# Expert matrices in 8 KB pieces, and a gathered block turned by sixteen 64x64 products with the identity

## What is computed

```python
def hier_moe(x, wg, bg, we, be, w1, w3, w2):
    ...   # route: each token gets 2 of 64 experts and two gates
    def expert_block(args):
        xb, e = args                      # xb: rows of tokens of expert e
        h = jax.nn.silu(xb @ w1[e]) * (xb @ w3[e])     # 1024 -> 256
        return h @ w2[e]                               # 256 -> 1024
    ys = lax.map(expert_block, (xs, blk_e)).reshape(R, D)
    out = jnp.zeros_like(xt).at[row_tok].add(ys * row_w[:, None])
```

## Time and profile before

| | |
|---|---|
| time, median of 3 runs | 3161.15 us (3158.59 to 3164.65) |
| span of the profiled execution | 3159.2 us |
| TensorE busy | 2918.6 us, 92% |
| TensorE weight loads busy | 2268.3 us, 72% |
| VectorE busy | 1399.3 us, 44% |
| ScalarE busy | 920.2 us, 29% |
| GpSimd busy | 608.3 us, 19% |
| DMA | 600.31 MB, mean 190 GB/s |

### The profile page before, as it was taken

One profiled execution on the slowest core, in us unless ns is written; L12 is line 12 of the kernel. 1 busy time (PEld: TensorE's weight loads), 2 busy tenths in 40 slices (PEclk: granted clock), 3 DMA queues, 4 the chain that ended last, 5 costly groups with the idle time before them and its releaser, 6 DMA issues.

```text
span 3159.2 us, 42475 instructions
## 1 busy us (share of the span) xinstructions
PE 2918.6 (92%) x17571; PEld 2268.3 (72%) x17571; DVE 1399.3 (44%) x2437; ACT 920.2 (29%) x1714; POOL 608.3 (19%) x534
## 2 busy tenths in 40 slices
PE   8999999999999999999999898888699997998884
PEld 7659999998888778888787555555577775555552
DVE  5634323343444543233544453323588844533234
ACT  4543313232222333142322121111335721211112
POOL 1404101120111131021100442222000002522220
PEclk9999999999999999999998899999899998999998
DMA  4012222222222222233225899999622139999996
GB/s 141 27 54 68 94 94 85 90 90 71 71 84 76 68 71 99 88 100 101 79 81 214 348 407 409 410 409 409 249 80 77 57 119 364 405 408 410 409 409 278
DMA packets 272213, 600.31 MB, mean 190 GB/s; under 512 B 32648, under 2 KB 177603, under 8 KB 255627
## 3 DMA queue, kind: packets, MB, share of 16 engines
q1 hardware_dynamic: 247552, 569.47, 47.9%
q0 software_dynamic: 23968, 27.93, 2.7%
q10 hardware_dynamic: 490, 0.08, 0.0%
HBM read 607.75 MB, written 39.89 MB: 205 GB/s over the span
## 4 chain that ended last, share of the span: by engine, by line
PE 86%; DVE 5%; issue 4%; ACT 2%; DMA 2%; POOL 1%; SPq 0%; ACTq 0%; DVEq 0%; POOLq 0%
PE ps L101 80%; PE ps L104 6%; DVE sb_tmpA L118 1%; DVE sb_arena L126 1%; DMA sb_arena<-in_exp_w_dram 1%; DVE sb_arena L118 1%; DVE sb_ws L118 1%; POOL sb_arena L118 0%; DMA sb_arena<-y_rows 0%; DVE sb_tmpA L129 0%; DMA sb_arena<-x_rows,sb_smallu 0%; ACT sb_arena L112 0%; ACT sb_hs L108 0%; ACT sb_hT L108 0%; DMA sb_arena<-in_x_dram 0%
## 5 line engine op out<-in xcount | busy, mean ns | idle before, releaser
L101 PE MATMUL ps<-sb_hs,sb_ws 128*128 128x264 f32 (+1 forms) x6384 | 1106.5, 335 | 17.2 <-ACT sb_hs L108 7.5
L101 PEld LDWEIGHTS ps<-sb_hs,sb_ws 128*128 128x128 f32 x6384 | 971.0, 190 | 148.2 <-issue 16.5
L118 DVE TENSOR_TENSOR sb_ws<-sb_ring,sb_ws 128x1024 fp32r<-128x1024 f32 x279 | 370.5, 1332 | 428.0 <-ACT sb_ws L112 427.5
L112 ACT CAST sb_ws<-sb_ring 128x1024 fp32r<-128x1024 f32 x279 | 290.8, 1046 | 333.6 <-PE ps L101 318.1
L101 PE MATMUL ps<-sb_arena 128*64 128x256 f32 (+18 forms) x1652 | 347.6, 420 | 26.6 <-issue 19.8
L101 PE MATMUL ps<-sb_br,sb_ws 128*128 128x264 f32 (+1 forms) x2304 | 367.4, 321 | 0.0
L101 PEld LDWEIGHTS ps<-sb_br,sb_ws 128*128 128x128 f32 x2304 | 332.4, 188 | 34.2 <-issue 0.5
L101 PE MATMUL ps<-sb_ring,sb_arena 128*64 128x256 f32 (+2 forms) x1506 | 284.0, 450 | 25.4 <-issue 22.6
L108 ACT ACTIVATE sb_arena<-ps 64x256 f32<-64x256 f32 (+6 forms) x188 | 73.8, 403 | 756.5 <-PE ps L101 733.8
L101 PEld LDWEIGHTS ps<-sb_arena 128*64 128x64 f32 (+6 forms) x1652 | 197.9, 160 | 128.7 <-issue 69.9
L104 PEld LDWEIGHTS ps<-sb_cst,sb_arena 128*128 128x128 f32 (+2 forms) x912 | 139.4, 209 | 170.6 <-DVE sb_arena L118 82.2
(11 more groups left out here) (198 smaller groups left out, 2602.7 us busy)
## 6 DMA issues: line engine op xcount, KB each, us to landing
sb_ring<-in_exp_w_dram SPq DMA_DIRECT2D x113, 1024.0 KB
sb_hx<-in_exp_w_dram SPq DMA_DIRECT2D x92, 1024.0 KB
sb_arena<-in_exp_w_dram SPq DMA_DIRECT2D x66, 1024.0 KB
sb_wx<-in_exp_w_dram SPq DMA_DIRECT2D x66, 1024.0 KB
sb_ring<-in_mlp_w_dram SPq DMA_DIRECT2D x64, 1024.0 KB
sb_hT<-in_exp_w_dram SPq DMA_DIRECT2D x47, 1024.0 KB
sb_ring<-in_od_w_in_dram SPq DMA_DIRECT2D x24, 1024.0 KB
sb_ring<-in_conv_w_in_dram SPq DMA_DIRECT2D x12, 1024.0 KB
```

The costliest lines, as they stand in the source:

```text
L101: return self.e.matmul(o, l, r, start=start, stop=stop, skip_group_check=True)
L112: return self.e.copy(o, i)
L118: return self.e.tensor_tensor(o, a, b, op)
```

## The change

The rows of the first and third matrices are dealt to the partitions differently: partition p now holds rows 8p to 8p+7, one run of 8 KB, in `moe_load` and in `over_sp`. To match, the turned block must have value 8p+o of a token in partition p. The values with p below 64 are in the upper 64 partitions of the gathered block and the others in the lower 64, so `turn_rows` takes for each o two 64x64 blocks (every eighth column) and multiplies each by the 64x64 identity: 8 x 2 ordinary products (`e.mm`) instead of 4 transposes (`e.tp`). `xgT`, `up_mm`, `columns_dve` and the loads of gains and biases follow the new order; their sizes stay.

```diff
--- before.py
+++ after.py
@@ -607,8 +607,8 @@
                     *grow_in.land())
             for l in range(2):
                 for i, name in enumerate(GROWS[0:2]):
-                    e.dma(sm[:, 384 + 16 * l + 8 * i:392 + 16 * l + 8 * i].rearrange("p (h o) -> p h o", h=2),
-                          A[name][l].rearrange("(h p o) -> p h o", h=2, o=4)).then_inc(*grow_in.land("all"))
+                    e.dma(sm[:, 384 + 16 * l + 8 * i:392 + 16 * l + 8 * i],
+                          A[name][l].rearrange("(p o) -> p o", o=8)).then_inc(*grow_in.land("all"))
             e.wait_ge(*dve_emptied["lut"])
             e.dma(Bd.rearrange("h (a b) -> h a b", a=2), lut).then_inc(*lut_out.land("all"))
 
@@ -2246,7 +2246,7 @@
 
         ar.at = base
         xg = ar.take(NG, 512)
-        xgT = ar.take(2, 4, 128)
+        xgT = ar.take(2, 8, CAP)
         hs = ar.take(2, 256)
         hhT = ar.take(2, 2, CAP)
         yy = ar.take(3, 512)
@@ -2363,7 +2363,7 @@
             if c == 2:
                 src, dst = W.rearrange("(p o) n -> p o n", o=2), v.rearrange("p (o n) -> p o n", o=2)
             else:
-                src, dst = W.rearrange("(h p o) n -> p h (o n)", h=2, o=4), v.rearrange("p (h n) -> p h n", h=2)
+                src, dst = W.rearrange("(p o) n -> p o n", o=8), v.rearrange("p (o n) -> p o n", o=8)
             e.dma(dst, src).then_inc(*wsignal(l, n).land(("moe", l, n)))
 
         for i in range(NSLOT):
@@ -2407,10 +2407,12 @@
             return q
 
         def turn_rows(e, units, key, src):
-            v = src.rearrange("s (p o) -> s o p", o=4)
+            v = src.rearrange("s (p o) -> s o p", o=8)
             u = units.take(e, key)
-            for o in range(4):
-                q = e.tp(u[:, 128 * o:128 * o + 128], v[:, o, :], ident)
+            for o in range(8):
+                for p in (0, CAP):
+                    q = e.mm(u[p:p + CAP, CAP * o:CAP * o + CAP], v[p:p + CAP, o, :], ident[p:p + CAP, p:p + CAP],
+                             True, True)
             return q
 
         def up_mm(e, units, key, xs, w1, w3):
@@ -2420,7 +2422,7 @@
             for k in range(8):
                 for c, w in enumerate((w1, w3)):
                     q = e.mm(u[CAP * c:CAP * c + CAP, 512 * c:512 * c + 256],
-                             xs[:, k % 4, CAP * (k // 4):CAP * (k // 4) + CAP], w[:, k, :], k == 0, k == 7)
+                             xs[:, k, :], w[:, k, :], k == 0, k == 7)
                     if k == 7:
                         ends.append(q)
             return ends
@@ -2656,9 +2658,8 @@
 
         def columns_dve(e, l, step, dst, src):
 
-            dst, src = (v.rearrange("p o (h s) -> p o h s", h=2) for v in (
-                dst, src[:, 0:512].rearrange("p (o n) -> p o n", o=4)))
-            g, b = (grid(GX[:, l, 8 * i:8 * i + 8], (1, 4), (4, 2), (0, CAP)) for i in range(2))
+            src = src[:, 0:512].rearrange("p (o s) -> p o s", o=8)
+            g, b = (grid(GX[:, l, 8 * i:8 * i + 8], (1, 8), (0, CAP)) for i in range(2))
             e.tt(dst, src, g, ALU.mult).then_inc(*step.mark())
             e.wait_ge(*step.now)
             return e.tt(dst, dst, b, ALU.add)
@@ -2772,11 +2773,7 @@
             x = e.e.value_load(over_of(l)[0:1, j:j + 1], min_val=0, max_val=63)
             for c in range(3):
                 W = EW[l][c][bass.ds(x, 1), :, :] if e.real else EW[l][c][0:1, :, :]
-                if c == 2:
-                    i = e.dma(ovw[:, c, :], W.rearrange("a (p o) n -> (a p) (o n)", o=2))
-                else:
-                    i = e.dma(ovw[:, c, :].rearrange("p (h m) -> p h m", h=2),
-                              W.rearrange("a (h p o) n -> p (a h) (o n)", h=2, o=4))
+                i = e.dma(ovw[:, c, :], W.rearrange("a (p o) n -> (a p) (o n)", o=2 if c == 2 else 8))
                 i.then_inc(*ovw_in[l].land(j))
 
         def over_pe(e, l, j):
```

## The result

The kernel with the change takes 3183.83 us (median of 4 runs, 3182.43 to 3185.06), the kernel before beside it 3160.02 (3158.59 to 3164.65): a ratio of 1.0071, 95% interval 1.0057 to 1.0084. The profiled executions say the same: 3181.8 us of span against 3159.2. The change makes the kernel slower by 0.7%.

A forecast was written before the change was run, and what follows sets the result against it. Transfers were taken to bound both expert loops, TensorE a close second. Per loop -9.1 + 0.7 = -8.4, two loops -16.8: span 3159.2 to 3142.4, plus 1.95 gives 3144.3 us; range 3138 to 3165.

The forecast's parts named there:

- What bounds the kernel: Both expert loops: weight transfers at 405 to 410 GB/s set the end; TensorE, 6.38 us per expert, is a close second.
- Part 1: First and third matrices' loads: 8 KB pieces save fixed packet cost, about 10 ns a packet, 9.1 us per loop.
- Rival B: Weight transfers: bytes, not packets, set the rate, so little or nothing is saved; 3162.6 down to 3156 us, chance 0.13.
- Part 2: Turn of the gathered block: sixteen products take 1.16 us, +0.48 per expert (6.86 us), hidden where transfers bind.
- so 0.06 for 64: Turn's weight loads: transposes' 0.12 us per 128 strided columns halved, giving 0.06 us per pair of product instructions.
- Rival C: Turn's loads: a step of 8 elements costs half as much again, 0.09 per pair; 3143 to 3160 us, chance 0.04.
- Rival A: Turn: row halves do not run side by side, TensorE binds at 7.82 us per expert; 3202.5 us, chance 0.16.
- The limit of TensorE: First loop: last up product could start at 1757.6 + 63c, c being us per expert; gain gone at 7.46.
- Part 3: Start of each loop: nothing hides the slower half-clock turn, costing 0.5 to 0.9 us, taken as 0.7 per loop.
- the forecast's own case: Whole kernel: pairs at 0.06 us, transfers still set the loops' ends; 3144.3 us, range 3139 to 3150, chance 0.67.
- One answer: Parts judged certain: VectorE's columns pass keeps 0.69 us; gain loads, overflow blocks and arena size cost nothing.

The follow-up runs named there:

- e1_pieces_only: Kernel before with only the 8 KB pieces of first and third matrices, four transposes kept: 3148.41 us, ratio 0.9956.
- e15: e16 with sixteen real products with the identity in place of its eight transposes, same 64 rows and 128 strided columns: 3641.06 us.
- e16: Changed kernel, but whole 4 KB rows gathered into 64 partitions, four blocks ahead, turned by eight transposes of 64 rows by 128 step-8 columns: 3183.25 us, ratio 1.0064.
- e3_step1: Changed kernel, but each 64x64 product takes 64 adjacent columns as weights in place of every eighth: 3152.54 us, ratio 0.9976.
- e9_halves_in_turn: Changed kernel with the sixteen products reordered, the eight of partitions 0-63 first, then those of 64-127: 3495.32 us in one run.
- e6_eight_transposes: Changed kernel with eight transposes of 128 rows by 64 step-8 columns in place of the products, plus VectorE passes: 3154.15 us, ratio 0.9981.

## Why the prediction was wrong

**What bounds the kernel**: right. Transfers came first, TensorE second; from 6.38 us per expert it had some 1.1 us to the point where the gain is gone (7.46 by the prediction's working). The change crossed that margin.

**Part 1**: right in kind, a fifth too large. 415 GB/s came where 417 was foretold, the weights' queue has 16988 packets in place of 26532. Before and after give one line: (279.7 - 181.7) / (7,223 - 4,579) = 0.037 ns per byte and 12 ns per packet, next to the prediction's 9.1 to 11.6. Alone it gave 14.8 of 18.2 us. Rival B is refuted. The Trainium skill, "DMA: Bandwidth & Descriptors", section "Why small descriptors are slow (HBM only)", has about 3 cycles per packet, an estimated 3.5 ns, which would have given 3.2 us per loop; e1_pieces_only gained 6.0 and 8.8.

**Part 2, the step that failed**: "so 0.06 for 64". The 0.12 us of a transpose was read rightly, but carried to another kind of instruction. Per strided column a real fp32 product pays twice what the transpose pays (e15 against e16); so a pair costs 0.12 and not 0.06, the turn 2.07 and not 1.16, an expert 7.77 and not 6.86. The other row used, 54 ns from the index products, has adjacent columns; e3_step1 shows that it was right for those (0.06 per pair, 6.78 us per expert). Rival C named the cause, the step of 8, and priced it at half as much again with a chance of 0.04; it is the true case with twice the price. Rival A gave the right pace (7.82) for a reason that e9_halves_in_turn refutes, and held the 0.16 that C should have had.

**The limit of TensorE**: 1757.6 + 63c was too strict. The first experts run into the routing's wait, which ends at the same time whatever the turn costs: the fifth up product starts at 1780.50 + 2.07 = 1782.57, before at 1782.50. Only 58 full steps follow: 1782.5 + 58c + 5.7 = 2238.9, measured 2238.73. So the loss began at 7.58 us in place of 7.46 and came to 22 us in place of rival A's 41.

**Part 3**: about right in the first loop. From the first turn's start to the first freed piece it takes 8.7 us (1744.26 to 1752.93), before 8.2 (1747.20 to 1755.38): +0.5 where 0.7 was foretold. In the second it is +0.2 (7.7 against 7.6). What it missed is that a slower turn costs transfers while TensorE eats its stock, since places come free later. From 1,757 to 1,850 us the rate is 400 GB/s before and 404 with the pieces alone; with step 1 and in the kernel after it is:

```profile
1757.00:1850.00 93.00, 90.19 (x992) 54.47 (x990) 55.13 (x110) 14.51 (x39) 42.54 (x32) 0.98 0.99 397
```

```profile
1757.00:1850.00 93.00, 91.19 (x883) 59.25 (x879) 46.40 (x101) 12.65 (x34) 39.74 (x29) 1.00 0.97 389
```

So e3_step1, which is the forecast's own case, came to 3152.5 and not to 3144.3: its loops gain 6.8 us, those of e1_pieces_only 14.8. The rates of the starting stretches account for some 1.5 us of the 4 per loop; the rest was not placed.

**One answer**: VectorE's first columns pass kept its 0.69 us, as said. The second one did not: from 1,757 to 1,900 us it takes 1.07 us in the mean of 19, against 0.69 before. Four of them last 2.4 us (3.4 in e3_step1), and each runs while GpSimd works on its passes of 128x1024, which before never met it. Nothing waits for them in the kernel after, so they cost no time here; in e6_eight_transposes such a meeting did.

## What to carry to other kernels

Before a strided operand becomes the weights of a real fp32 product, look at how many bytes lie between its columns: up to 8 bytes it cost nothing here, at 16 and more each 64-column load took 0.12 us, and a product needs two. Take the price of a load only from rows of the same instruction, the same type and the same step; a transpose with the identity is a different one. And where the second engine needs only 1 us per step less than the first, a change that helps the first has to be priced on the second before anything else.

## What the chip showed that was not expected

- Weight loads of fp32 products: 134 ns at steps of 4 and 8 bytes, 171 at 12, 211 at 16, 213 at 32; the step between pairs is 0.06, 0.06, 0.09, 0.12 and 0.12 us.
- The same strided operand costs 0.94 ns per column or less as a transpose's weights and 1.88 as a product's.
- Two tiles in opposite corners (partitions 0-63 and 64-127, columns likewise) load and run side by side into one PSUM bank, 0.06 us for both. The Trainium skill, "TensorEngine Tiling (Array Packing)", section "Gotcha 1: PSUM Pressure", has it that different row tiles cannot access one bank at the same time; for these corners no run shows such a cost.
- The granted clock, which is at its upper level (1.00, 2.4 GHz) all through this stretch in the kernel after, was at the lower one (0.50, 1.2 GHz) for a part of it where the turn's strided loads come one after the other: the means are 0.85 in e9_halves_in_turn and 0.79 in e15_same_loads_as_products (1,760 to 1,900 us), with TensorE busy 139 of 140 us in both. In e9 it was 1.00 from 1877.44 to 1880.00 us, all of it in the turn, and 0.52 from 1880.00 to 1883.50, from the turn's end into the up products.
- VectorE's pass over 128x512 from SBUF to SBUF, 0.69 us otherwise, takes 2.4 to 3.4 us where it meets a GpSimd pass over 128x1024 (2.5 us each), in every such meeting of the kernel after and of e3_step1 in both loops.
